# Stick-breaking attention in a decoder layer: q and k loaded by partition halves, and another order of VectorE's work in a step

## The chip, the cores and the metric

The kernel runs on one core of one Trainium2 chip. The metric is the device time of the whole layer in microseconds (us), from the first instruction to the last. Times are given as the median of several executions; a profile is of one execution.

## The reference, cut to what matters

The layer has an input projection, a pooling mixer and an attention side by side, an output projection and a gated MLP. Only the attention is touched by the change. It has 8 heads of 64 columns over 2048 positions, and for each head computes:

```
z[t, s]  = (q[t] . k[s]) / 8                                   (scores)
A[t, s]  = sigmoid(z[t, s]) * prod over s < j < t of (1 - sigmoid(z[t, j]))   for s < t, else 0
out[t]   = sum over s of A[t, s] * v[s]
```

Everything is float32. The products that need the precision are made with operands split into a high and a low half (`hi` is the value rounded to the matmul type, `lo` is the rest), so that q, k, v and the weights each come in two halves.

## The kernel before, in words

The kernel works in phases, one after the other, with a barrier between two: values (projection of v), projections (pool, q, k, written to the DRAM scratch `qk_scratch` as a high and a low half of 128 rows each, two heads to a tile), attention, mix (output projection), up and down (the MLP). The change lies in `phase_attention` alone.

**Tiles of a head.** q_hi and q_lo (lines 556, 557) hold q's high and low half, each twice: on partitions 0 to 63 and again on 64 to 127. k_both (line 558) holds k's high half on partitions 0 to 63 and its low half on 64 to 127, so that one matmul over 128 partitions sums both. v_both holds v with its halves side by side. There are two buffers of each, one for the even head of a pair (e = 0) and one for the odd (e = 1).

**Loads.** `load_head` (line 620) issues four DMAs on SyncE's queue: q_hi and q_lo, whose source is the same 64 rows twice (line 624 puts a leading dimension of 2 with a step of 0 ahead of them), k_both, whose source has a leading dimension of 2 (high, low) over 64 rows, and v_both, whose source has 128 rows. The first head is loaded in three parts (4, 4 and 8 tiles of 128 positions, `head_parts`). After the start SyncE's queue has: the three parts of head (0, 0), head (0, 1), sixteen pieces of w_out for the next phase (line 638 to 641, two buffers, each piece waits until the one two before it has been used by GpSimd), and then in turn, when the last product of a head is done (line 644), the load of the head two later into the same buffers and the store of the finished head's output. TensorE waits at line 763 or 765 for all of a head's or a part's DMAs before it makes the first scores with them.

**Units and steps.** A head has 16 query tiles of 128; tile q needs keys up to itself, cut in units of up to 512 keys, taken from the diagonal backwards. So tile q has q // 4 + 1 units; the first has 128, 256, 384 or 512 keys, the others 512. A head has 40 units (28 of 512, 4 each of 384, 256 and 128), the kernel 320. Each engine goes through the same numbered steps, one for each unit u, and works in step u on several units at once, with fixed lags (line 545). All waits are semaphores; within an engine the order is as written:

- TensorE in step u (line 793): the scores of u (q_hi and q_lo against k_both, and on a diagonal unit a mask product) into one of 4 PSUM banks z_ps; then `turn`, the transposes of unit u - 4's weights into one of 2 banks wT_ps, which waits until VectorE has taken the low half of unit u - 6 out of that bank (line 777); then `values`, the products of unit u - 6 with v, which wait for the same low half (line 784).
- ScalarE in step u (line 657): beta = sigmoid(z), then 1 - beta = sigmoid(-z) in place (line 663), then the high half of wT of unit u - 4 (line 669), which waits for its transposes and for the values of unit u - 6, since wT has 2 buffers.
- VectorE in step u (line 711): the low half of wT of unit u - 5 (line 719), the running product over the keys of unit u with the scan instruction (line 738), which starts from the last value of the scan before and waits for the result of line 663; and after the last unit of a query tile the row sum, which adds the two halves of the output (line 748, unit u - 6). In the second head of the first pair it also has a copy of a piece of w_out in every other step (line 709).
- GpSimd in step u (line 682): weight = beta * running product of unit u - 1 (line 692).

Of the kernel before, what the change touches and what calls it, by code (L numbers as in the profile page):

```python
# [8 lines left out]
ALU = mybir.AluOpType  # L9
# [3 lines left out]
P = 128  # L13
# [4 lines left out]
HEAD_DIM = 64  # L18
# [8 lines left out]
def done(step, lead=LEAD):  # L27
    return step + 1 + lead


def freed(step, ring=LEAD, lead=LEAD):
    return step + 1 + lead - ring
# [26 lines left out]
def as_f32(tile):  # L59
    return tile.bitcast(F32)  # L60
# [470 lines left out]
def phase_attention(nc, a, c, s, wide, bridge):  # L531
# [8 lines left out]
    heads = a["d_attn"] // HEAD_DIM  # L540
    scale = HEAD_DIM ** -0.5
    lead = 8
    z_ring, stick_in, weight_ring, wT_ring = 4, 5, 4, 2

    weight_lag, turn_lag, hi_lag, lo_lag, values_lag, read_lag = 1, 4, 4, 5, 6, 6

    units = [(e, q, k * BANK, min((q + 1) * P - k * BANK, BANK), k == q // per, k == 0)
             for e in range(2) for q in range(tiles) for k in range(q // per, -1, -1)]
# [3 lines left out]
    with ExitStack() as stack:  # L552
# [3 lines left out]
        q_hi = [n.sb(f"q_hi{i}", [P, seq], F32R) for i in range(2)]  # L556
        q_lo = [n.sb(f"q_lo{i}", [P, seq], F32R) for i in range(2)]
# [19 lines left out]
            n.sem(x) for x in ("z_done", "rest_done", "beta_done", "stick_done", "weight_done",  # L577
                               "wT_turned", "wT_hi_done", "wT_lo_done", "pv_done", "o_read"))

        pairs = heads // 2  # L580
        last_read = max(weight_lag, turn_lag, hi_lag, lo_lag, values_lag, read_lag)

        def steps(eng, step):
# [29 lines left out]
        with nc.Block() as block:  # L613

            @block.sync
            def _(sp):
                for sem in mixed_out:
                    sp.sem_inc(sem, 16)

                def load_head(pair, e, sem, first=0, end=tiles):  # L620

                    half, cols = slice(e * HEAD_DIM, (e + 1) * HEAD_DIM), slice(first * P, end * P)
                    for hi_lo, dst in enumerate((q_hi, q_lo)):
                        twice = s["qk"][pair, hi_lo, half, cols].unsqueeze(0).broadcast_to([2, HEAD_DIM, (end - first) * P])
                        sp.dma_start(as_f32(dst[e][:, cols]), twice).then_inc(sem, 16)
                    sp.dma_start(as_f32(k_both[e][:, cols]), s["qk"][pair + heads // 2, :, half, cols]).then_inc(sem, 16)
                    sp.dma_start(as_f32(v_both[e][:, first:end, :, :]), s["v"][pair * 2 + e][:, first:end, :, :]).then_inc(sem, 16)

                def store_head(pair, e):
                    sp.wait_ge(o_read, done((pair * 2 + e + 1) * tiles - 1, lead))  # L630
                    row = (pair * 2 + e) * HEAD_DIM
                    sp.dma_start(s["merged"][bass.ds(a["d_pool"] + row, HEAD_DIM), :], mixed[e][0:HEAD_DIM, :]).then_inc(mixed_out[e], 16)
                    sp.dma_start(s["attn_low"][bass.ds(row, HEAD_DIM), :], mixed[e][HEAD_DIM:P, :]).then_inc(mixed_out[e], 16)

                for first, end, sem in head_parts:
                    load_head(0, 0, sem, first, end)
                load_head(0, 1, head_in[1])
                for m in range(2 * a["kc"]):
                    if m >= 2:
                        sp.wait_ge(wo_done, m - 1)  # L640
                    sp.dma_start(wo_f[:, m % 2, :], wo_rows[m // 2][:, (m % 2) * BANK:(m % 2 + 1) * BANK]).then_inc(wo_in[m % 2], 16)
                with sp.Fori(0, heads // 2 - 1) as i:
                    for e in range(2):
                        sp.wait_ge(pv_done, done(i * total + (e + 1) * per_head - 1, lead))
                        load_head(i + 1, e, head_in[e])
                        store_head(i, e)
                for e in range(2):
                    store_head(heads // 2 - 1, e)
                for e in range(2):
                    sp.wait_ge(mixed_out[e], stored(heads // 2, 32))  # L650
# [46 lines left out]
            @block.vector  # L697
            def _(dve):
                for sem in (stick_done, lo_done, o_read):
                    dve.sem_inc(sem, lead)  # L700
                for i in range(2):
                    dve.memset(stick[i][:, seq:seq + 1], 1.0).then_inc(one_done, 1)
                dve.wait_ge(one_done, 2)

                def high_wo(m):

                    k, h = m // 2, m % 2
                    dve.wait_ge(wo_in[h], 16 * (k + 1))
                    dve.tensor_copy(wide[h][:, k, :], wo_f[:, h, :]).then_inc(wo_hi_done, 1)

                def step(i, u, behind):
                    if wo_part(i, u) is not None:
                        high_wo(wo_part(i, u))
                    if behind(lo_lag):
                        v, t = behind(lo_lag)
                        w = units[v][3]
                        dve.wait_ge(hi_done, done(t, lead))
                        dve.wait_ge(pv_done, freed(t, wT_ring, lead))
                        dve.tensor_tensor(wT[v % wT_ring][:, 0:w // P, 1, :], wT_ps[v % wT_ring][:, 0:w].rearrange("p (b k) -> p b k", k=P),  # L719
                                          as_f32(wT[v % wT_ring][:, 0:w // P, 0, :]), ALU.subtract).then_inc(lo_done, 1)  # L720
                    if u < total:
                        e, q, key, w, first, _ = units[u]
                        t = i * total + u
                        dve.wait_ge(rest_done, done(t, lead))
                        if first:

                            if e or q >= 2:
                                before = last_unit[(e, q - 2)] if q >= 2 else last_unit[(0, tiles - 2 + q)]
                                dve.wait_ge(weight_done, done(i * total + before, lead))
                            elif not isinstance(i, int):  # L730
                                dve.wait_ge(weight_done, done(i * total + (last_unit[(1, tiles - 2 + q)] - total), lead))
                            start = 1.0
                        else:
                            dve.wait_ge(stick_done, freed(t, 1, lead))
                            start = stick[q % 2][:, col(q, key) + w:col(q, key) + w + 1]
                        at = col(q, key)
                        backwards = z_ps[u % z_ring][:, 0:w][:, ::-1]
                        dve.tensor_tensor_scan(stick[q % 2][:, at:at + w][:, ::-1], backwards, beta[u % stick_in][:, 0:w], start,  # L738
                                               ALU.mult, ALU.bypass).then_inc(stick_done, 1)

                    if behind(read_lag) and units[behind(read_lag)[0]][5]:
                        v, t = behind(read_lag)
                        e, q = units[v][0:2]
                        dve.wait_ge(pv_done, done(t, lead))
                        if q == 0:
                            dve.wait_ge(mixed_out[e], stored(i if u >= read_lag else i - 1, 32))

                        dve.tensor_reduce(mixed[e][:, q * P:(q + 1) * P], o_ps[q % 2][:, :, :].rearrange("e h k -> e k h"), AX.X,
                                          ALU.add).then_inc(o_read, 1)

                steps(dve, step)

            @block.tensor
            def _(pe):
# [3 lines left out]
                def scores(i, u):  # L758
                    e, q, key, w, first, _ = units[u]
                    if isinstance(i, int) and i == 0 and e == 0:  # L760
                        for start, _, sem in head_parts:
                            if first and q == start:
                                pe.wait_ge(sem, 16 * 4)
                    elif u % per_head == 0:
                        pe.wait_ge(head_in[e], 16 * 4 * i + 16 * 4)
                    pe.wait_ge(stick_done, freed(i * total + u, z_ring, lead))
                    for k, half in enumerate((q_hi, q_lo)):
                        m = pe.matmul(z_ps[u % z_ring][:, 0:w], half[e][:, q * P:(q + 1) * P], k_both[e][:, key:key + w],  # L768
                                      start=(k == 0), stop=(k == 1))
                        if first and k == 0:  # L770
                            pe.matmul(z_ps[u % z_ring][:, w - P:w], c["ident_r"][:, :], c["not_before"][:, :], start=False, stop=False)
                    m.then_inc(z_done, 1)
# [740 lines left out]
```

## Time and profile before

| what | value |
|---|---|
| median of 3 runs | 2896.52 us (2894.82 to 2897.53) |
| profiled execution, its own time | 2898.21 us |
| its span | 2896.4 us |
| busy: TensorE matmul, VectorE, ScalarE, GpSimd | 86%, 49%, 37%, 15% of the span |
| mean granted TensorE clock | 0.951 |
| attention: first matmul, end of the last row sum | 447.30 us, 1150.83 us |

The busy shares are means over phases with different limits. In the attention (from 424 to 1158 us) no engine is busy over the whole stretch; the rows further down tell why. PE is TensorE's matmul, PEld its weight load, DVE VectorE, ACT ScalarE, POOL GpSimd, and SPq SyncE as the issuer of DMAs. PEclk is the granted clock of TensorE, 1.00 for 2.4 GHz and 0.50 for 1.2 GHz.

### The profile page before, as it was taken

Reading aid. Unit: us, or ns where it says so; the run is one execution under the profiler, and the core shown is the slowest. Engines: PE = TensorE matmul, PEld = TensorE weight load, DVE = VectorE, ACT = ScalarE, POOL = GpSimd, SP = SyncE. Lnnn points to the kernel's source line nnn. Section 1 sums busy time; section 2 is a strip of 40 time slices with the busy share of each in tenths; the row PEclk is TensorE's granted clock in tenths of the full one; section 3 lists DMA queues with packets and bytes.
Section 4 is the critical chain, followed back from the end, with each engine's and each line's share of the span. In section 5 each row is a group of like instructions: output and inputs, shape, how many; then the busy total and the mean of one; then the engine's idle time right before and its main releaser. Section 6 shows DMA issues by size and latency. Waiting matters only on the chain. (4 is left out here: it accounts for less than half of the span.)

```text
span 2896.4 us, 36114 instructions
## 1 busy us (share of the span) xinstructions
PE 2498.8 (86%) x11941; PEld 2049.1 (71%) x11941; DVE 1406.3 (49%) x1876; ACT 1075.8 (37%) x1828; POOL 433.9 (15%) x408
## 2 busy tenths in 40 slices
PE   6899983655767776899699999999999999999997
PEld 5677862544555555787588888888888878787876
DVE  4424113775888888677333333333334333434343
ACT  4311112664666676455222222222222222323322
POOL 0000001563444444223000000000000000101011
PEclk9999996897999999899799999999999999999999
DMA  8913331211222121578811111111111114545453
GB/s 240 270 39 115 119 103 64 72 64 69 69 68 68 68 69 30 185 215 260 279 51 50 43 52 47 44 54 46 45 54 45 54 61 172 189 142 188 149 182 115
DMA packets 247504, 307.57 MB, mean 106 GB/s; under 512 B 10688, under 2 KB 175224, under 8 KB 242808
## 3 DMA queue, kind: packets, MB, share of 16 engines
q1 hardware_dynamic: 242808, 289.80, 31.3%
q0 software_dynamic: 4608, 16.78, 1.5%
q8 instruction: 33, 0.54, 0.1%
q14 instruction: 55, 0.45, 0.1%
HBM read 195.39 MB, written 94.37 MB: 100 GB/s over the span
## 5 line engine op out<-in xcount | busy, mean ns | idle before, releaser
L692 POOL TENSOR_TENSOR weight<-beta,stick 128x512 f32<-128x512 f32 (+3 forms) x320 | 305.2, 957 | 791.9 <-ACT beta L662 466.0
L1234 DVE SCALAR_TENSOR_TENSOR conv<-value_ps,taps,conv 128x512 f32<-128x512 f32 (+2 forms) x176 | 131.2, 745 | 370.5 <-ACT conv L1194 370.5
L779 PE MATMUL wT_ps<-ident,weight 128*128 128x128 f32 x1088 | 184.7, 287 | 99.9 <-DVE wT L719 96.5
L768 PE MATMUL z_ps<-k_both,q_hi 128*128 128x512 f32 (+3 forms) x320 | 120.8, 377 | 171.3 <-DMA v_both<-v_scratch 171.3
L1337 POOL TENSOR_TENSOR y<-y,x 128x1024 f32<-128x1024 f32 x16 | 38.9, 2432 | 1450.2 <-DVE y L1396 1449.9
L779 PEld LDWEIGHTS wT_ps<-ident,weight 128*128 128x128 f32 x1088 | 125.7, 145 | 180.5 <-issue 160.1
L506 PE MATMUL out_ps<-hT,w_hi 128*128 128x512 f32 x768 | 240.0, 394 | 9.8 <-DVE w_lo L440 9.8
L738 DVE TENSOR_TENSOR_SCAN stick<-z_ps,stick,beta 128x512 f32<-128x512 f32 x192 | 244.4, 1273 | 5.0 <-ACT z_ps L663 4.0
L662 ACT ACTIVATE beta<-z_ps 128x512 f32<-128x512 f32 (+3 forms) x320 | 170.9, 534 | 172.9 <-PE z_ps L768 169.1
L1260 PE MATMUL gate_ps<-wide,wu_hi 128*128 128x512 f32 x704 | 217.9, 391 | 2.9 <-DMA wide<-h2T_scratch 2.9
L1260 PE MATMUL value_ps<-wide,wu_hi 128*128 128x512 f32 x704 | 216.8, 389 | 0.0
L1234 DVE SCALAR_TENSOR_TENSOR conv<-gate_ps,taps,conv 128x512 f32<-128x512 f32 (+2 forms) x176 | 131.1, 745 | 172.3 <-ACT conv L1194 172.3
L789 PE MATMUL o_ps<-wT,v_both 128*128 128x256 f32 x1088 | 213.0, 311 | 1.0 <-DVE wT L719 1.0
L1194 ACT ACTIVATE conv<-value_ps,taps 128x512 f32<-128x512 f32 x88 | 68.7, 781 | 390.7 <-PE value_ps L1260 390.7
L669 ACT ACTIVATE wT<-wT_ps 128x512 fp32r<-128x512 f32 (+3 forms) x320 | 171.1, 535 | 104.5 <-PE o_ps L789 102.3
L719 DVE TENSOR_TENSOR wT<-wT_ps,wT 128x512 fp32r<-128x512 f32 (+3 forms) x320 | 188.8, 590 | 16.8 <-ACT wT L669 13.9
L768 PEld LDWEIGHTS z_ps<-k_both,q_hi 128*128 128x128 f32 x320 | 63.4, 198 | 173.8 <-issue 98.8
L506 PEld LDWEIGHTS out_ps<-hT,w_hi 128*128 128x128 f32 x768 | 145.1, 189 | 42.3 <-DVE w_lo L440 10.2
L738 DVE TENSOR_TENSOR_SCAN stick<-z_ps,beta 128x128 f32<-128x128 f32 (+3 forms) x128 | 104.1, 813 | 143.9 <-ACT z_ps L663 143.1
L663 ACT ACTIVATE z_ps<-z_ps 128x512 f32<-128x512 f32 (+3 forms) x320 | 172.6, 539 | 0.0
L789 PEld LDWEIGHTS o_ps<-wT,v_both 128*128 128x128 f32 x1088 | 155.6, 197 | 1.4 <-DVE wT L719 1.2
L1260 PEld LDWEIGHTS gate_ps<-wide,wu_hi 128*128 128x128 f32 x704 | 132.8, 189 | 30.9 <-issue 3.3
(164 smaller groups left out, 5262.8 us busy)
## 6 DMA issues: line engine op xcount, KB each, us to landing
wu_f<-in_w_up SPq DMA_DIRECT2D x44, 512.0 KB, 5.6
f_scratch<-f SPq DMA_DIRECT2D x88, 256.0 KB, 2.4
bridge<-in_w_down SPq DMA_DIRECT2D x44, 512.0 KB, 3.5
bridge<-f_scratch SPq DMA_DIRECT2D x88, 256.0 KB, 3.7
wd_f<-in_w_down SPq DMA_DIRECT2D x44, 512.0 KB, 3.6
xt<-in_x SPq DMA_DIRECT2D x16, 512.0 KB, 5.7
hT<-h_hi SPq DMA_DIRECT2D x16, 512.0 KB, 4.6
hT<-h_lo SPq DMA_DIRECT2D x16, 512.0 KB, 5.5
```

The costliest lines, as they stand in the source:

```text
L506: m = pe.matmul(out_ps[half + j][:, :], w[slot][:, k, :], hT[h][:, k, j * BANK:(j + 1) * BANK], start=(k == 0 and t == 0), stop=(k == kc - ...
L662: act.activation(beta[u % stick_in][:, 0:w], z_ps[u % z_ring][:, 0:w], ACT.Sigmoid, scale=scale).then_inc(beta_done, 1)
L663: act.activation(z_ps[u % z_ring][:, 0:w], z_ps[u % z_ring][:, 0:w], ACT.Sigmoid, scale=-scale).then_inc(rest_done, 1)
L669: act.activation(wT[v % wT_ring][:, 0:w // P, 0, :], wT_ps[v % wT_ring][:, 0:w].rearrange("p (b k) -> p b k", k=P), ACT.Copy).then_inc(hi_ ...
L692: pool.tensor_tensor(weight[v % weight_ring][:, 0:w], beta[v % stick_in][:, 0:w], stick[q % 2][:, at:at + w], ALU.mult).then_inc(weight_do ...
L719: dve.tensor_tensor(wT[v % wT_ring][:, 0:w // P, 1, :], wT_ps[v % wT_ring][:, 0:w].rearrange("p (b k) -> p b k", k=P), as_f32(wT[v % wT_ri ...
L738: dve.tensor_tensor_scan(stick[q % 2][:, at:at + w][:, ::-1], backwards, beta[u % stick_in][:, 0:w], start, ALU.mult, ALU.bypass).then_inc ...
L768: m = pe.matmul(z_ps[u % z_ring][:, 0:w], half[e][:, q * P:(q + 1) * P], k_both[e][:, key:key + w], start=(k == 0), stop=(k == 1))
L779: m = pe.transpose(wT_ps[u % wT_ring][:, b * P:(b + 1) * P], weight[u % weight_ring][:, b * P:(b + 1) * P], c["ident"][:, :])
L789: m = pe.matmul(o_ps[q % 2][:, :, :], v_both[e][:, key // P + b, :, :], wT[u % wT_ring][:, b, :, :], start=(first and b == 0), stop=(last ...
L1234: dve.scalar_tensor_tensor(out=out, in0=ps[h][:, g * BANK - back + skip:(g + 1) * BANK - back], scalar=column(kind, h, slot), in1=out, op0 ...
L1260: m = pe.matmul(ps[h][:, g * BANK:(g + 1) * BANK], w[slot][:, h, k, :], hT[x][g][:, k, :], start=(k == 0 and t == 0), stop=(k == kc - 1 an ...
```

## The change

Two things are changed. In `load_head` the q_hi, q_lo and k_both loads are split in two: each DMA now fills 64 partitions from 64 rows, so that a head or part of a head has 7 DMAs where it had 4 (6 of q and k, and v as before), issued as k, q_hi, q_lo for the lower partitions, the same for the upper ones, then v. The waits of TensorE count 7 in place of 4. And VectorE's order within a step is scan of unit u, low half of unit u - 5, row sum of unit u - 6, where it was low half, scan, row sum.

```
-        pairs = heads // 2
+        pairs, loads = heads // 2, 7
...
                     half, cols = slice(e * HEAD_DIM, (e + 1) * HEAD_DIM), slice(first * P, end * P)
-                    for hi_lo, dst in enumerate((q_hi, q_lo)):
-                        twice = s["qk"][pair, hi_lo, half, cols].unsqueeze(0).broadcast_to([2, HEAD_DIM, (end - first) * P])
-                        sp.dma_start(as_f32(dst[e][:, cols]), twice).then_inc(sem, 16)
-                    sp.dma_start(as_f32(k_both[e][:, cols]), s["qk"][pair + heads // 2, :, half, cols]).then_inc(sem, 16)
+                    for part in range(2):
+                        rows = slice(part * HEAD_DIM, (part + 1) * HEAD_DIM)
+                        sp.dma_start(as_f32(k_both[e][rows, cols]), s["qk"][pair + heads // 2, part, half, cols]).then_inc(sem, 16)
+                        for hi_lo, dst in enumerate((q_hi, q_lo)):
+                            sp.dma_start(as_f32(dst[e][rows, cols]), s["qk"][pair, hi_lo, half, cols]).then_inc(sem, 16)
                     sp.dma_start(as_f32(v_both[e][:, first:end, :, :]), s["v"][pair * 2 + e][:, first:end, :, :]).then_inc(sem, 16)
...
                 def step(i, u, behind):
                     if wo_part(i, u) is not None:
                         high_wo(wo_part(i, u))
-                    if behind(lo_lag):
-                        v, t = behind(lo_lag)
-                        w = units[v][3]
-                        dve.wait_ge(hi_done, done(t, lead))
-                        dve.wait_ge(pv_done, freed(t, wT_ring, lead))
-                        dve.tensor_tensor(wT[v % wT_ring][:, 0:w // P, 1, :], wT_ps[v % wT_ring][:, 0:w].rearrange("p (b k) -> p b k", k=P),
-                                          as_f32(wT[v % wT_ring][:, 0:w // P, 0, :]), ALU.subtract).then_inc(lo_done, 1)
                     if u < total:
...
                         dve.tensor_tensor_scan(stick[q % 2][:, at:at + w][:, ::-1], backwards, beta[u % stick_in][:, 0:w], start,
                                                ALU.mult, ALU.bypass).then_inc(stick_done, 1)
 
+                    if behind(lo_lag):
+                        v, t = behind(lo_lag)
+                        w = units[v][3]
+                        dve.wait_ge(hi_done, done(t, lead))
+                        dve.wait_ge(pv_done, freed(t, wT_ring, lead))
+                        dve.tensor_tensor(wT[v % wT_ring][:, 0:w // P, 1, :], wT_ps[v % wT_ring][:, 0:w].rearrange("p (b k) -> p b k", k=P),
+                                          as_f32(wT[v % wT_ring][:, 0:w // P, 0, :]), ALU.subtract).then_inc(lo_done, 1)
                     if behind(read_lag) and units[behind(read_lag)[0]][5]:
...
-                                pe.wait_ge(sem, 16 * 4)
+                                pe.wait_ge(sem, 16 * loads)
                     elif u % per_head == 0:
-                        pe.wait_ge(head_in[e], 16 * 4 * i + 16 * 4)
+                        pe.wait_ge(head_in[e], 16 * loads * i + 16 * loads)
```

## Rows read from the trace of the kernel before

**Rows 1.** TensorE's waits from 430 to 1160 us: total us, times, longest us

```profile
PE z_ps L768 <- DMA v_both<-v_scratch: 171.3, 10, 45.6
PE wT_ps L779 <- DVE wT L719: 96.5, 166, 1.3
```

**Rows 2.** Stretches: length; busy PE, PEld, DVE, ACT, POOL (instructions); PEclk, DMA share, GB/s

```profile
545.00:562.00 17.00, 0.81 (x6) 0.61 (x5) 2.10 (x3) 0.60 (x1) 1.09 (x1) 0.61 0.12 50
...
730.00:748.00 18.00, 14.96 (x99) 11.75 (x100) 18.00 (x25) 15.86 (x32) 11.03 (x11) 1.00 0.52 149
...
1100.00:1140.00 40.00, 32.87 (x218) 25.81 (x217) 39.72 (x55) 33.73 (x72) 23.20 (x24) 1.00 0.00 0
...
1142.00:1149.00 7.00, 4.69 (x36) 4.16 (x36) 4.85 (x8) 2.99 (x5) 2.19 (x2) 1.00 0.00 1
```

**Rows 3.** Timeline, TensorE's first matmul behind a wait for loads: start, us, [idle before]

```profile
447.30 0.47 PE L768 MATMUL z_ps<-k_both,q_hi 128*128 128x128 f32 x1 [24.88 <-DMA v_both<-v_scratch]
...
679.60 0.47 PE L768 MATMUL z_ps<-k_both,q_hi 128*128 128x128 f32 x1 [45.58 <-DMA v_both<-v_scratch]
...
758.43 0.47 PE L768 MATMUL z_ps<-k_both,q_hi 128*128 128x128 f32 x1 [9.96 <-DMA v_both<-v_scratch]
```

**Rows 4.** Timeline of SyncE's queue: the first loads of heads (0, 0) and (1, 0)

```profile
427.73 0.67 SPq L625 DMA_DIRECT2D q_hi<-qk_scratch  x1
...
612.73 0.58 SPq L625 DMA_DIRECT2D q_hi<-qk_scratch  x1
```

**Rows 5.** DMA issues of the page: count, KB each, us from issue to landing

```profile
bridge<-in_w_out SPq DMA_DIRECT2D x16, 256.0 KB, 2.6
```

**Rows 6.** VectorE's groups from 430 to 1160 us: busy us, mean ns | idle before

```profile
L738 DVE TENSOR_TENSOR_SCAN stick<-z_ps,stick,beta 128x512 f32<-128x512 f32 x192 | 244.4, 1273 | 5.0 <-ACT z_ps L663 4.0
L719 DVE TENSOR_TENSOR wT<-wT_ps,wT 128x512 fp32r<-128x512 f32 (+3 forms) x320 | 188.8, 590 | 16.8 <-ACT wT L669 13.9 <-issue 2.9
L738 DVE TENSOR_TENSOR_SCAN stick<-z_ps,beta 128x128 f32<-128x128 f32 (+3 forms) x128 | 104.1, 813 | 143.9 <-ACT z_ps L663 143.1
```

**Rows 7.** Timeline 801 to 805 us: from one low half to the scan that hangs on it

```profile
801.28 0.68 DVE L719 TENSOR_TENSOR wT<-wT_ps,wT 128x512 fp32r<-128x512 f32 x1
...
802.10 0.63 PE L779 MATMUL wT_ps<-ident,weight 128*128 128x128 f32 x4 [0.65 <-DVE wT L719]
...
802.49 0.71 PE L789 MATMUL o_ps<-wT,v_both 128*128 128x256 f32 x4
...
803.28 0.39 PE L768 MATMUL z_ps<-k_both,q_lo 128*128 128x512 f32 x1
803.30 0.60 ACT L669 ACTIVATE wT<-wT_ps 128x512 fp32r<-128x512 f32 x1 [0.64 <-PE o_ps L789]
...
804.27 0.61 ACT L663 ACTIVATE z_ps<-z_ps 128x512 f32<-128x512 f32 x1
...
804.91 1.28 DVE L738 TENSOR_TENSOR_SCAN stick<-z_ps,stick,beta 128x512 f32<-128x512 f32 x1 [0.27 <-ACT z_ps L663]
```

**Rows 8.** The same at narrower units: low half and second Sigmoid, twice

```profile
797.55 0.66 DVE L719 TENSOR_TENSOR wT<-wT_ps,wT 128x512 fp32r<-128x512 f32 x1
...
800.21 0.28 ACT L663 ACTIVATE z_ps<-z_ps 128x128 f32<-128x128 f32 x1
...
806.42 0.68 DVE L719 TENSOR_TENSOR wT<-wT_ps,wT 128x512 fp32r<-128x512 f32 x1
...
809.01 0.59 ACT L663 ACTIVATE z_ps<-z_ps 128x512 f32<-128x512 f32 x1
```

**Rows 9.** Timeline of VectorE at the end of the attention

```profile
1140.61 1.27 DVE L738 TENSOR_TENSOR_SCAN stick<-z_ps,stick,beta 128x512 f32<-128x512 f32 x1
1141.81 0.66 DVE L719 TENSOR_TENSOR wT<-wT_ps,wT 128x512 fp32r<-128x512 f32 x1
1142.39 1.27 DVE L738 TENSOR_TENSOR_SCAN stick<-z_ps,stick,beta 128x512 f32<-128x512 f32 x1
...
1150.41 0.42 DVE L748 TENSOR_REDUCE mixed<-o_ps 128x128 f32<-128x256 f32 x1 [0.83 <-PE o_ps L789]
```

## The prediction, made before the changed kernel was run

> **What bounds the kernel now.** I read the page first: no engine is full over the span, so the question is what bounds the attention, the one phase touched. It runs from the first matmul at 447.30 to the end of the last row sum at 1150.41 + 0.42 = 1150.83, that is 703.5 us [rows 3, 9]. TensorE's waits in it come next: 171.3 us in ten waits for a head's loads (the wait is put down to v_both, the last of the DMAs), and 96.5 us in 166 short waits for VectorE's low half [rows 1]. The stretches tell the two states apart. Inside a head VectorE is busy for 39.72 of 40 us: it is the bound. Between heads nearly nothing runs, the DMA share is 0.12 and 50 GB/s move: 0.12 is two of sixteen DMA engines. Where v's load of 128 rows comes into play the share rises to 0.52 and 149 GB/s [rows 2]. So the q and k loads, whose source has a leading dimension of 2, run on two engines, and a head is late because of them. The first wait is 24.88 us, one is 45.58, and one of 9.96 stands for five that lie between 9.6 and 11.7 [rows 3].
>
> **The loads, part by part.** Removed: three DMAs per head with a leading 2. Added: six with 64 rows each. I expect these to spread as v's does. A head is 4 MiB; even at the 149 GB/s of a mixed stretch [rows 2] that is 28 us, and they are issued a whole head (65 us or more) ahead. So the seven waits behind the first three vanish. The 45.58 is longer because its loads go out only at 612.73, behind the w_out pieces [rows 3, 4]; head (0, 1) went on for 21 us from there (679.60 - 45.58 = 634.02), and for some 26 with the longer steps below, so a load of 20 to 28 us is hidden or nearly so. At the start SyncE issues seven DMAs of about 0.7 us from 427.73 [rows 4], so the last goes out at 432.6; a load of 256 KB lands after 2.6 us when alone [rows 5], and 1 MiB at 149 GB/s takes 7. I take 437 for the first matmul, with 434 (all at once) and 447.3 (no gain) as its ends. The second and third part may still be waited for by some 2 us together (from nothing to what they cost before). SyncE's three extra issues per head are 2 us; behind them only the store of the head before is queued, whose reader is the next phase, so that costs nothing. Without the gaps TensorE also stays at 2.4 GHz: the clock reads 0.61 in a wait, 1.00 inside a head [rows 2]. By the loads alone the attention would be about 180 us shorter: 146.4 of waits after the first, 10 at the start, and some 3 us of refill and half clock behind each of eight.
>
> **VectorE's order.** The work is the same, its place is not, and this is the part that costs. TensorE in step u waits for the low half of unit u - 6 before its transposes, then does the values, then the scores of unit u + 1. ScalarE's two Sigmoids follow, then scan u + 1. One such chain reads: low half ends at 801.96, transposes 802.10, values 802.49 to 803.20, scores end 803.67, the high half starts at 803.30 and the two Sigmoids behind it end at 804.88, and the scan starts at 804.91 [rows 7]. That is 2.95 us from low half to scan; I use 2.93, which the places with full units round out to. Before, the low half comes first in a step, so the chain from low half (step u - 1) to scan (u + 1) and to the next low half behind it (step u + 2) spans three steps: (2.93 + 1.2 + 0.67) / 3 = 1.6 us a step, under VectorE's own 1.78 (1140.61 to 1142.39) [rows 9]. That is why VectorE is full. Afterwards the low half of unit u - 6 comes at the end of step u - 1 and the low half behind scan u + 1 in that same step: the chain spans two steps. A full unit then takes (2.93 + 1.20 + 0.66) / 2 = 2.39 us, with the scan's start to the low half's start 1.20 [rows 9]. VectorE idles 0.6 us a step, into which the row sums and the w_out copies fall, so they cost nothing as long as that idle time is there.
>
> For narrower units: means over all 320 are 1.09 for the scan (244.4 + 104.1 over 320), less 0.08 of overlap, and 0.59 for the low half [rows 6]. The chain is 2.28 long where the scan's unit has 128 keys (800.49 less 798.21) and 2.50 where the transposed one has (809.60 less 807.10) [rows 8], so a block of 128 keys is worth about 0.22 and 0.14, and 0.12 more for the values (estimate from their 0.71 for four). A mean unit has 3.4 blocks of 4: 2.93 - 0.6 x 0.48 = 2.64. Mean pitch (2.64 + 1.01 + 0.59) / 2 = 2.12, or 84.8 us a head. If narrow units relieved nothing it would be 40 x 2.39 = 95.8. Steps of even and odd number form two interlaced chains, and the slower one sets the pace; in 24 of the 40 steps the narrow unit always falls on the same of them and relieves the other less. I take 86.5, near the lower end since both get part of the relief.
>
> **The sum.** 437 + 1.6 (scores to first scan, from 803.28 to 804.88 [rows 7]) + 8 x 86.5 = 692 + 8.4 (last scan's start to the end [rows 9]) + 2 of load waits = 1141.0, against 1150.8: 10 us shorter. The first steps have no low half yet, which saves about what the half clock at the start costs. The later phases wait for the attention's last store and are as before. 2898.2 - 10 = 2888 for the profiled execution; the median of the runs lies 1.7 lower: 2886.5. A measurement here can tell about 0.2% (5.8 us) from no change.
>
> **A rule that speaks against it.** The trace has the former loads on two engines' worth of share [rows 2]. The Trainium skill, "DMA: Bandwidth & Descriptors", rules for kernel authors, says of two transfers to disjoint partition halves not to bother, since both spread over all sixteen engines anyway and take turns. By that rule splitting would bring nothing; the row shows that these were not spread over sixteen, which the rule takes for granted.
>
> **The rivals.**
> - **The order costs more (slower).** The place is the same two-step chain. If the two chains disturb each other, so that narrow units relieve little, a head takes 92 us, 736 in all: 44 more than my sum, 34 slower than before, 2931. It decides from 88 us a head. For it: the offset between the chains has only about 1.2 us of play (4.79 - 2 x 1.78), less than a 128-key unit takes off at once. Against: what one chain loses so need not be on the slower one.
> - **The order costs nothing.** If my chain is wrong and VectorE stays full, the loads' 180 us are all gained: 2717. Against: TensorE waits 166 times for just this low half [rows 1].
> - **The loads are no faster.** Halves share the engines as before, and a head still comes in slowly. With heads 21 us longer, the five waits of about 10 us (52 together) vanish anyway, 45.6 becomes 25, and the first ones stay: 146.4 - 52 - 20 = 74 of waits are left beside 702 of steps, 73 us slower, 2970. The rule quoted would lead here. Against: the share of 0.12 beside the 0.52.
> - **The clock falls.** TensorE's busy share in a head goes from 0.82 to about 0.62. The lowest stretch at clock 1.00 has 0.67 [rows 2]. If it dropped for half of the time, transposes, values and scores would take some 1.7 us more in those chains, 0.85 a step over 160 steps: 136 slower than my sum, 3023. Against: at half clock the share would be high again.
>
> **How the numbers follow.** The forecast has 0.65, the costlier order 0.19, the free order 0.06, slow loads 0.05, the clock 0.05. Inside the forecast, 84.8 a head, a start at 434 and a chain 0.05 shorter give 35 us less than before (2862), 88 to 89 a head some 5 to 10 more: of its 0.65, 0.48 is faster, 0.12 the same, 0.05 slower. The costlier order gives 0.03 the same and 0.16 slower. Faster 0.48 + 0.06 = 0.54, same 0.15, slower 0.05 + 0.16 + 0.05 + 0.05 = 0.31. The range 2860 to 2930 takes in the forecast and nearly all of the costlier order, some 0.8.
>
> **What would show it.** Right: no wait over 3 us for v_both after the first; a DMA share well over 0.12 while q and k load; the first matmul near 437; VectorE idle by 0.4 to 0.6 us before most scans, put down to ScalarE's second Sigmoid; scan to scan two steps on 4.8 us for full units; 86 to 87 us a head. Wrong: VectorE busy for over 95% of a head (the order is free), waits of 10 us or more left (the loads), PEclk under 1 inside a head, or a head of 90 us or more.

## The result, and the profile after

The changed kernel takes 2929.61 us (median of four runs, 2927.26 to 2932.60) against 2896.89 us before: a ratio of 1.0115 with a 95% interval of 1.0097 to 1.0132, so about 33 us slower. The forecast was 10 us faster. The profiled execution took 2927.26 us with a span of 2925.6.

TensorE's waits from 424 to 1260 us in the changed kernel come first (total us, times, longest us), as in [rows 1]:

```profile
PE wT_ps L780 <- DVE wT L740: 240.5, 232, 2.4
...
PE z_ps L769 <- DMA v_both<-v_scratch: 15.6, 2, 13.4
```

The load waits have fallen from 171.3 us to 15.6, nearly all of it the first one. The short waits for the low half have risen from 96.5 us in 166 to 240.5 in 232: 144 us more. So the loads did what was expected, and the time has moved to the other wait.

VectorE's groups in the same stretch (busy us, mean ns | idle before), as in [rows 6]:

```profile
L732 DVE TENSOR_TENSOR_SCAN stick<-z_ps,stick,beta 128x512 f32<-128x512 f32 x192 | 245.7, 1280 | 110.5 <-ACT z_ps L664 110.1
L740 DVE TENSOR_TENSOR wT<-wT_ps,wT 128x512 fp32r<-128x512 f32 (+3 forms) x320 | 187.1, 585 | 2.6 <-ACT wT L670 2.6
L732 DVE TENSOR_TENSOR_SCAN stick<-z_ps,beta 128x128 f32<-128x128 f32 (+3 forms) x128 | 105.0, 820 | 82.5 <-ACT z_ps L664 79.6 <-POOL weight L693 2.6
```

The durations are those of before; new is the idle time ahead of the long scans, 110.5 us where it was 5.0, released by ScalarE's second Sigmoid. VectorE no longer bounds the heads.

The stretches of the changed kernel (columns as in [rows 2]), first one while q, k and v load beside the first steps, then nearly the whole attention, then a single fall of the clock with what lies ahead of it:

```profile
437.00:461.00 24.00, 16.53 (x70) 13.52 (x70) 15.79 (x24) 13.47 (x33) 9.87 (x12) 0.64 1.02 219
...
461.00:1177.00 716.00, 479.30 (x2848) 382.73 (x2847) 533.98 (x754) 434.42 (x926) 314.98 (x325) 0.92 0.21 54
...
822.00:824.00 2.00, 0.44 (x3) 0.29 (x3) 2.00 (x4) 1.19 (x3) 0.72 (x1) 1.00 0.98 197
824.00:825.50 1.50, 0.94 (x6) 0.51 (x6) 1.50 (x3) 0.80 (x3) 0.95 (x2) 1.00 1.03 208
825.60:829.00 3.40, 3.40 (x15) 3.12 (x16) 1.90 (x4) 1.63 (x4) 1.28 (x2) 0.51 0.99 207
```

In the first stretch the DMA share is full and 219 GB/s move, where the same loads ran at 0.12 and 50 GB/s. In the long one TensorE is busy for 0.67 of the time, and its clock is not 1.00 but 0.92 on average: again and again it falls to 1.2 GHz for a few us. If 0.92 is the mean of times at 1.00 and at 0.50, about 115 of the 716 us were at 1.2 GHz (an estimate from that row). In the fall shown, TensorE worked for 0.44 of the 2 us from 822.0 and for 0.94 of the next 1.5, and the clock then reads 0.51 from 825.6 to 829.0. The timelines of the engines at that place (start, us, [idle before <- releaser]):

```profile
824.71 0.66 DVE L740 TENSOR_TENSOR wT<-wT_ps,wT 128x512 fp32r<-128x512 f32 x1
...
825.52 0.96 PE L780 MATMUL wT_ps<-ident,weight 128*128 128x128 f32 x4 [0.58 <-DVE wT L740]
826.13 1.20 PE L790 MATMUL o_ps<-wT,v_both 128*128 128x256 f32 x4
...
828.93 0.59 ACT L664 ACTIVATE z_ps<-z_ps 128x512 f32<-128x512 f32 x1
...
829.55 1.22 DVE L732 TENSOR_TENSOR_SCAN stick<-z_ps,beta 128x512 f32<-128x512 f32 x1 [1.66 <-ACT z_ps L664]
```

This is the chain of [rows 7] at half clock: transposes 0.96 where they took 0.63, values 1.20 where they took 0.71. From the end of the low half (825.37) to the end of the second Sigmoid (829.52) it is 4.15 us, where it was 2.92 (801.96 to 804.88); some 0.1 of it is a mask product, since this unit lies on the diagonal. The attention ends with the last row sum:

```profile
1182.31 0.42 DVE L749 TENSOR_REDUCE mixed<-o_ps 128x128 f32<-128x256 f32 x1 [0.83 <-PE o_ps L790]
```

1182.73, against 1150.83 before: 31.9 later. The two profiled executions differ by 29.1 us and the medians by 32.7, so the attention holds the whole loss within what one execution tells. The first matmul is at 436.07, so 11.2 us earlier than before and within 1 us of the forecast. From there to the last row sum it is 746.7 us, where the forecast had 704.0 (437 to 1141.0), 5.3 us more for each of the eight heads.

### The profile page after: what moved, and what is told of

The parts are those of the page before. It is cut to its first block and busy times, and to the rows that moved or that the text cites. A ratio compares the mean times of both kernels' runs of the same rounds, so it can differ in the third digit from the quotient of the medians.

```text
span 2925.6 us, 36165 instructions
## 1 busy us (share of the span) xinstructions
PE 2541.8 (87%) x11941; PEld 2076.9 (71%) x11941; DVE 1419.6 (49%) x1876; ACT 1083.3 (37%) x1828; POOL 433.8 (15%) x408
## 5 line engine op out<-in xcount | busy, mean ns | idle before, releaser
L780 PE MATMUL wT_ps<-ident,weight 128*128 128x128 f32 x1088 | 201.5, 306 | 242.6 <-DVE wT L740 240.5
L780 PEld LDWEIGHTS wT_ps<-ident,weight 128*128 128x128 f32 x1088 | 132.3, 154 | 339.7 <-issue 311.6
L732 DVE TENSOR_TENSOR_SCAN stick<-z_ps,stick,beta 128x512 f32<-128x512 f32 x192 | 245.7, 1280 | 110.5 <-ACT z_ps L664 110.1
L790 PE MATMUL o_ps<-wT,v_both 128*128 128x256 f32 x1088 | 229.0, 329 | 0.7 <-DVE wT L740 0.7
L790 PEld LDWEIGHTS o_ps<-wT,v_both 128*128 128x128 f32 x1088 | 169.5, 212 | 1.4 <-DVE wT L740 1.1
L1261 PEld LDWEIGHTS value_ps<-wide,wu_hi 128*128 128x128 f32 x704 | 132.0, 188 | 27.5
L506 PE MATMUL out_ps<-hT,w_lo 128*128 128x512 f32 x384 | 150.2, 391 | 0.0
```

Source lines behind the costliest of these rows:

```text
L506: m = pe.matmul(out_ps[half + j][:, :], w[slot][:, k, :], hT[h][:, k, j * BANK:(j + 1) * BANK], start=(k == 0 and t == 0), stop=(k == kc - ...
L780: m = pe.transpose(wT_ps[u % wT_ring][:, b * P:(b + 1) * P], weight[u % weight_ring][:, b * P:(b + 1) * P], c["ident"][:, :])
L790: m = pe.matmul(o_ps[q % 2][:, :, :], v_both[e][:, key // P + b, :, :], wT[u % wT_ring][:, b, :, :], start=(first and b == 0), stop=(last ...
L1261: m = pe.matmul(ps[h][:, g * BANK:(g + 1) * BANK], w[slot][:, h, k, :], hT[x][g][:, k, :], start=(k == 0 and t == 0), stop=(k == kc - 1 an ...
```

## The experiments

Theory A: the split takes away the waits for loads, and the new order makes the chain from a low half to the scan that hangs on it span two steps in place of three. Theory B: TensorE's longer idle times in that chain let its clock fall, which makes the chain longer still. Theory C: what helps in the loads is that no leading dimension of 2 is left, not that there are halves. The rivals stand with each run. All ratios are against the kernel before, run on the same chip.

**Each part alone.** The loads alone are the changed kernel with the low half back ahead of the scan; the order alone is the kernel before with the low half behind the scan.

```
 # loads only, against the changed kernel       # order only, against the kernel before
+  if behind(lo_lag): ... low half               -  if behind(lo_lag): ... low half
   if u < total: ... scan                           if u < total: ... scan
-  if behind(lo_lag): ... low half               +  if behind(lo_lag): ... low half
```

> The changed kernel with VectorE's old order back (low half, scan, row sum): only the split loads are left. Theory A (the loads' waits are removed, and the new order costs a two-step chain through TensorE and ScalarE): VectorE is the bound again with about 65 us a head, no wait for loads over 3 us after the first, 2717 us (2705 to 2735). Rival (six smaller DMAs in a burst slow the engines, and the order is harmless): the heads stay above 85 us and the kernel above 2850.

> The kernel before with VectorE's new order, loads as before. Theory A: a head's steps take 88 to 92 us in place of 65, the five waits of 10 us vanish behind the longer heads, the 45.6 us wait shrinks by 20 to 25, the ones of the first head stay; 2975 to 2995 us, so about 90 slower than before. Rival (the order costs nothing by itself): 2897. If the two parts simply added up, this run and the loads alone would have to sum to the changed kernel's +33; by theory A they do not, since the longer heads hide waits that the split would otherwise remove.

The loads alone give 2737.52 us, a ratio of 0.9461 (0.9445 to 0.9476): 159 us faster. The order alone gives 3003.99 us, 1.0377 (1.0359 to 1.0394): 107 us slower. So each part has its effect by itself and theory A stands in both; both sizes were a little off (2717 and 2975 to 2995 expected). The two effects do not add up: -159 + 107 = -52, but together they give +33. TensorE's waits with the order alone tell why:

```profile
PE wT_ps L779 <- DVE wT L739: 236.0, 228, 2.2
PE z_ps L768 <- DMA v_both<-v_scratch: 90.6, 5, 38.0
```

Of the 171.3 us of load waits [rows 1] only 90.6 are left although the loads are the slow ones: the longer heads hide 81 us of them. That is nearly the 85 us by which the sum misses. What the new order costs is partly paid with waits that were there anyway; once the loads are fast, its full price shows: 2929.6 against 2737.5, 192 us.

With the loads alone, VectorE is again the bound, and the clock is whole. TensorE's waits for a low half are then 106.3 us, where the changed kernel has 240.5:

```profile
PE wT_ps L780 <- DVE wT L720: 106.3, 183, 2.0
...
461.00:980.00 519.00, 414.74 (x2791) 333.28 (x2790) 510.00 (x745) 419.58 (x912) 310.54 (x320) 1.00 0.28 75
```

**The distance in steps, not the place in the code.** Two variants of the changed kernel keep the low half behind the scan, and change only which unit's low half it is.

```
-  weight_lag, turn_lag, hi_lag, lo_lag, values_lag, read_lag = 1, 4, 4, 5, 6, 6
+  weight_lag, turn_lag, hi_lag, lo_lag, values_lag, read_lag = 1, 4, 4, 6, 6, 7     (unit u - 6)
+  weight_lag, turn_lag, hi_lag, lo_lag, values_lag, read_lag = 1, 4, 4, 4, 6, 6     (unit u - 4)
```

> The changed kernel, the low half still behind the scan, but that of unit u - 6 in place of u - 5, and the row sum of unit u - 7 in place of u - 6. The place in the step is the new one, the distance from a low half to the scan that hangs on it is three steps again. Theory A (the length of the chain in steps is all that counts): as with the loads only, 2717 us (2705 to 2740), VectorE full in a head. Rival (the place behind the scan itself costs, for example because the scan then holds TensorE up): about 2930.

> The changed kernel, low half behind the scan as in it, but that of unit u - 4 in place of u - 5. Behind scan u - 1 comes then the low half of unit u - 5, as in the kernel before, and the chain spans three steps. (The run with unit u - 6 went the wrong way: its chain spans one step.) Theory A (the length of the chain in steps counts, not the place in the code): 2737 us as with the loads only, within 8 us. Rival (the place behind the scan costs): 2930.

The first of the two is a miss of mine that turned out the most telling run. It took 3854.60 us, 1.3311 (1.3289 to 1.3333). I had counted the wrong way: a larger lag means that the low half of a unit comes later, so that of unit u - 6 stands in step u itself, and the chain spans one step. Its VectorE timeline:

```profile
1002.33 0.96 DVE L732 TENSOR_TENSOR_SCAN stick<-z_ps,beta 128x384 f32<-128x384 f32 x1 [3.88 <-ACT z_ps L664]
1003.21 0.66 DVE L740 TENSOR_TENSOR wT<-wT_ps,wT 128x512 fp32r<-128x512 f32 x1
1007.54 1.28 DVE L732 TENSOR_TENSOR_SCAN stick<-z_ps,stick,beta 128x512 f32<-128x512 f32 x1 [3.67 <-ACT z_ps L664]
```

Every scan waits nearly 4 us for the chain of the low half just ahead of it. The clock is down as well, to 0.52 at a busy share of 0.47:

```profile
461.00:2100.00 1639.00, 769.25 (x2862) 597.67 (x2863) 545.96 (x763) 460.03 (x930) 318.44 (x327) 0.52 0.09 24
```

The second puts the low half of unit u - 5 behind scan u - 1, where it was before the change, with the code in the new place: 2733.10 us, 0.9438 (0.9420 to 0.9457), the same as the loads alone (the intervals overlap). So the place behind the scan costs nothing. What counts is over how many steps the same chain is spread: three, 2733 to 2738 us; two, 2930; one, 3855. Both three-step kernels beat the kernel before and the changed one.

**The clock.** A product that nothing reads is added to each step of TensorE, behind the scores, where it would otherwise wait for the low half. It goes into the score bank of the next unit, which that unit's scores overwrite.

```
                    if u < total:
                        scores(i, u)
+                   if u < total:
+                       pe.wait_ge(stick_done, freed(i * total + u + 1, z_ring, lead))
+                       for _ in range(2):                      # 1 in the next two, 128 columns in the last
+                           pe.matmul(z_ps[(u + 1) % z_ring][:, :], c["ident_r"][:, :], k_both[units[u][0]][:, 0:BANK], start=True, stop=True)
```

> The changed kernel, with two products of 512 columns more per step on TensorE, written into the score bank of the next unit before its own scores overwrite it; they stand behind the scores, where TensorE waits for the low half. Theory B (some 4 us a head are lost because TensorE, busy for 0.66 of the time, falls to 1.2 GHz for a few us again and again): PEclk 1.00 through the heads, a head 88 us, 2898 us (2890 to 2910, a little more where the added work holds up the transposes at narrow units). Rival (the clock costs nothing, the two chains disturb each other): the clock is back, the time is 2930 or more.

> The changed kernel with one added product of 512 columns per step on TensorE in place of two. Theory B (the clock): half of the added work raises the busy share by about 0.1 in place of 0.2; some of the drops to 1.2 GHz are left, 2900 to 2915 us. If the gain of the two products came from something else than the clock, the drops would be as many as in the changed kernel and the time 2930.

> The changed kernel with one added product of 128 columns per step, a quarter of the work of the smaller filler. Theory B: it raises TensorE's busy share by about 0.03 only; part of the drops to 1.2 GHz stay, the time lies between 2899 and 2930, about 2918. Rival (any product in the gap will do, for example because TensorE's next instruction starts sooner): 2900.

> Control for the added products: the kernel with the split loads only and VectorE's old order, with the same one product of 512 columns per step. Here the clock is 1.00 in the heads already. Theory B (the added product helped only by the clock): no gain, 2737 us or up to 20 more, since TensorE has less room (its busy share goes from 0.82 to about 0.9). If it gains 20 us or more here too, the added product helps by something else and theory B falls.

Two products of 512 columns: 2903.61 us, 1.0022 (1.0012 to 1.0032). One: 2899.41 us, 1.0008 (0.9999 to 1.0018). One of 128 columns: 2919.05 us, 1.0073 (1.0056 to 1.0090). So a kernel that does more work on TensorE is up to 30 us faster than the changed kernel. The stretches of the attention, in the order 128 columns, 512, twice 512 (each from its own profile):

```profile
461.00:1170.00 709.00, 485.46 (x3143) 419.75 (x3142) 533.31 (x754) 432.97 (x925) 314.19 (x324) 0.94 0.21 55
```

```profile
461.00:1150.00 689.00, 504.53 (x3147) 392.36 (x3145) 534.07 (x754) 431.45 (x922) 314.17 (x323) 0.99 0.22 57
```

```profile
461.00:1150.00 689.00, 563.17 (x3444) 443.87 (x3443) 532.86 (x752) 433.13 (x920) 314.82 (x323) 1.00 0.21 56
```

| run | TensorE busy share | PEclk | us |
|---|---|---|---|
| changed kernel | 479.30 / 716 = 0.67 | 0.92 | 2929.61 |
| + 128 columns | 485.46 / 709 = 0.68 | 0.94 | 2919.05 |
| + 512 columns | 504.53 / 689 = 0.73 | 0.99 | 2899.41 |
| + 2 x 512 columns | 563.17 / 689 = 0.82 | 1.00 | 2903.61 |

Time falls as the clock rises, and stops falling when the clock is nearly whole; the second product of 512 columns brings nothing more (the ratios' intervals, 1.0012 to 1.0032 and 0.9999 to 1.0018, overlap, so that it costs is not shown). In the kernel with three steps, where the clock is whole without it, the same product of 512 columns gives 2744.72 us, 0.9477 (0.9461 to 0.9493): no gain, the time is that of the loads alone or a few us more. So the added product helps where the clock falls, and no help by anything else shows: theory B, worth a net 30 of the changed kernel's us. Each expectation held, but for the single product of 512 columns: it was already enough, where 2900 to 2915 and some falls left were expected.

**What it is about the loads.** Two variants of the loads alone: v's load in two halves of the partitions too (8 DMAs), and k_both back in one DMA whose source has (high, low) as its leading dimension (6 DMAs).

```
+                    for part in range(2):
+                        rows = slice(part * HEAD_DIM, (part + 1) * HEAD_DIM)
+                        sp.dma_start(as_f32(v_both[e][rows, first:end, :, :]), s["v"][pair * 2 + e][rows, first:end, :, :]).then_inc(sem, 16)
...
-                        sp.dma_start(as_f32(k_both[e][rows, cols]), s["qk"][pair + heads // 2, part, half, cols]).then_inc(sem, 16)
+                    sp.dma_start(as_f32(k_both[e][:, cols]), s["qk"][pair + heads // 2, :, half, cols]).then_inc(sem, 16)
```

> The kernel with the split loads only, and v's load split by halves of the partitions too (8 DMAs per head or part). Theory C (what helped q and k was to be rid of the leading dimension of 2, and halves by themselves bring nothing, since v's load of 128 rows ran on all engines before): 2737 us, within 4. Rival (smaller DMAs are faster by themselves): the first matmul some us earlier than 437 and 2733 or less.

> The kernel with the split loads only, but k_both in one DMA again, with its leading dimension of 2 (high, low), which is no repetition of the same rows. Theory C: this one runs on two engines, at about 53 GB/s, so it takes 20 us for a head; hidden behind a head of 65 us, seen only at the start: first matmul 439 to 443, 2741 us (2737 to 2752). DMA share near 0.12 for a while after q and v have landed. Rival (only the repeated q rows were slow): first matmul at 437 and a short burst at a share of 0.5 and more.

The stretch shown below is from the run with k in one DMA. With v in halves: 2741.46 us, 0.9456 (0.9441 to 0.9472), the same as the loads alone. Halves by themselves bring nothing for a load that was spread already. With k in one DMA: 2772.02 us, 0.9572 (0.9554 to 0.9591), 35 us slower than the loads alone. Theory C holds in kind: there is again a time in which a leading dimension of 2, here without a repeated row, has the queue for itself, on two engines' worth of share:

```profile
590.00:600.00 10.00, 1.73 (x12) 1.12 (x10) 4.68 (x7) 2.45 (x5) 3.27 (x3) 0.79 0.13 53
```

The size was missed, 2741 was expected, since I had taken one megabyte in 20 us to be hidden everywhere. It isn't at two places. SyncE issues head (1, 0)'s loads behind the w_out pieces, and at the start the parts follow one another. SyncE's queue and TensorE's first matmul of that head:

```profile
573.75 0.62 SPq L627 DMA_DIRECT2D k_both<-qk_scratch  x1
...
607.29 0.47 PE L769 MATMUL z_ps<-k_both,q_hi 128*128 128x128 f32 x1 [14.90 <-DMA v_both<-v_scratch]
```

Only 18.6 us after k's issue TensorE was ready for it (607.29 - 14.90 = 592.4), and it had to wait until 33.5 us after. All four waits of this run together are 46.7 us, against 16.3 with the loads alone.

## Why the prediction was wrong

- **What bounds the kernel before, and the loads: right.** Two engines' worth of share for the q and k loads; the first matmul at 436.07 (437 forecast); no wait over 3 us after the first; 219 GB/s while loading. The gain by the loads alone was put at 180 us and was 159. Of the three terms 146.4 of later waits and 10 at the start (11.6 measured: that run's first matmul is at 435.67) make up nearly all; of the third, some 3 us of refill behind each of eight waits (24 in all), little was there: the attention ended at 989.91, 160.9 us earlier than before, which leaves 2.9. That TensorE's idle time in such a wait already holds what VectorE has left to do is a likely reason, but argued.
- **The order: right in kind.** The two-step chain through TensorE and ScalarE is what holds VectorE up, as the idle time ahead of its scans and the runs with one, two and three steps show. The chain at full clock was also well sized: between two loop ends a head with one added product takes 87.7 us (below), where 86.5 was forecast.
- **The step that failed: "without the gaps TensorE also stays at 2.4 GHz".** I charged the new order only with its wait at full clock, and put the clock into a rival with a chance of 0.05, since the lowest share seen at clock 1.00 was 0.67 over 7 us [rows 2]. The share did come to 0.67, and the clock still fell to 0.92 on average. A mean share hides how the work lies: TensorE's waits for a low half go up to 2.4 us, where before none was over 1.3 [rows 1]. Which pattern of idle times brings the clock down is not shown: with the loads alone the longest such wait was 2.0 us and the clock stayed at 1.00, but all of them together were 106.3 us in place of 240.5. The forecast's attention ended at 1141.0, the measured one at 1182.73: 41.7 later. With one added product it ends at 1154.85, so the clock is 28 of these, net of what the product itself costs.
- **The remaining 14 us.** VectorE's timeline in that run, at the first scan of 256 keys of heads (2, 0), (2, 1) and (3, 0), and at the end:

```profile
794.12 0.69 DVE L732 TENSOR_TENSOR_SCAN stick<-z_ps,beta 128x256 f32<-128x256 f32 x1 [2.00 <-ACT z_ps L664]
...
881.82 0.69 DVE L732 TENSOR_TENSOR_SCAN stick<-z_ps,beta 128x256 f32<-128x256 f32 x1 [0.98 <-ACT z_ps L664]
...
974.09 0.69 DVE L732 TENSOR_TENSOR_SCAN stick<-z_ps,beta 128x256 f32<-128x256 f32 x1 [2.01 <-ACT z_ps L664]
...
1154.43 0.42 DVE L749 TENSOR_REDUCE mixed<-o_ps 128x128 f32<-128x256 f32 x1 [0.84 <-PE o_ps L790]
```

  From 794.12 to 881.82 it is 87.7 us, from 881.82 to 974.09 92.3. The second contains the end of a pair, where all engines jump back in their loops, which the first doesn't: 4.6 us more, twice in the kernel, 9 us that the sum had at nothing. The jump may not be all of these 4.6. At the first of the two places TensorE stands still for 2.98 us for no wait that the profile shows, and the clock is at 1.2 GHz from before it resumes until 4.8 us after:

```profile
787.50:794.30 6.80, 4.78 (x21) 4.42 (x21) 1.19 (x3) 1.71 (x5) 0.70 (x2) 0.50 0.02 6
...
789.52 0.47 PE L769 MATMUL z_ps<-k_both,q_hi 128*128 128x128 f32 x1 [2.98 <-issue]
```

  How the 4.6 divide between the jump and the half clock behind it was not measured. The other 5 are a head of somewhat over 86.5.
- **The rival that came true in time** was the costlier order, 2931 by its working. Its mechanism was not the main one: it wanted 92 us a head because two interlaced chains spoil each other's relief. With one added product, away from the loop ends, the heads are near 88, so that part is about 1 us a head; the clock and the loop ends made the rest. It was priced right for a reason that holds only in small part.
- **The free order and the slow loads** are out: VectorE idles, and the loads are fast. The Trainium skill, "DMA: Bandwidth & Descriptors", rules for kernel authors, says not to bother with two transfers to disjoint partition halves. v's load agrees: with it in halves the kernel took 2741.46 us, with the loads alone 2737.52. For q and k the runs say otherwise (159 us faster), since their one transfer had a leading dimension of 2 and moved 50 to 53 GB/s.

## What to carry to other kernels

When an instruction is moved within a step of a software pipeline (engines working on several units at once, with fixed lags), count over how many steps the chain of waits through the other engines is spread before and after, and divide its length by that; here one step fewer took VectorE from the bound to 0.6 us of idle time a step (189.7 us over 320 steps) and cost 192 us, more than the fast loads had gained. Before costing an added wait on TensorE's path, ask too what clock the engine will have with that idle time, and try a cheap product in the gap. A DMA whose access pattern begins with a dimension of 2 is worth splitting whenever the share of the DMA engines stands at an eighth while something waits for it, and two changes that touch the same wait must be measured one by one.

## What the runs showed of the hardware that was not expected

- TensorE's clock fell to 1.2 GHz in the middle of a steady pipeline, behind idle times of no more than 2.4 us (the longest wait of the changed kernel for a low half), and was back within a few us. One product of 512 columns a step, put into the idle time, turned 30 us of loss back. With the loads alone such waits went up to 2.0 us and the clock stayed whole, so the length of a single wait does not tell.
- A load with a leading dimension of 2 ran on two DMA engines' worth of share whether the 2 was a repetition (q) or two different blocks (k): 0.12 to 0.13 and 50 to 53 GB/s, against 1.02 and 219 GB/s for the split ones.
- The end of a pair, where each engine jumps back in its loop, is not free even where no load is waited for. In the loads-only run VectorE idles there without a releaser, and in the run with two added products TensorE does:

```profile
848.38 0.69 DVE L720 TENSOR_TENSOR wT<-wT_ps,wT 128x512 fp32r<-128x512 f32 x1 [1.59 <-issue]
```

```profile
969.87 0.32 PE L769 MATMUL z_ps<-k_both,q_hi 128*128 128x128 f32 x1 [3.15 <-issue]
```

  With VectorE itself as the bound a pair's end costs 1.6 us, with a chain over three engines 4.6, and there a time at 1.2 GHz follows TensorE's idle 3 us, which may be part of the 4.6. Whether the jumps also add up along the chain was not tried.
